# FoX attention over the paged past: K tiles read by indirect transfers on GpSimd, in one order with V

## The reference

```python
past = (_gather_pages(cache_fox_k[i], page_table),
        _gather_pages(cache_fox_v[i], page_table),
        _gather_pages(cache_fox_logf[i], page_table))
...
k_all = jnp.concatenate([pk.astype(k.dtype), k], axis=1)
v_all = jnp.concatenate([pv.astype(v.dtype), v], axis=1)
...
s = jnp.einsum('bqhd,bkhd->bhqk', q_i, k).astype(f32) * ATTN_SCALE
s = s + jnp.transpose(cq_i, (0, 2, 1))[..., None] - cum_k_t[:, :, None, :]
s = jnp.where(k_idx[None, None, None, :] <= pos_i[None, None, :, None], s, -jnp.inf)
pr = jax.nn.softmax(s, axis=-1)
return jnp.einsum('bhqk,bkhd->bqhd', pr.astype(v.dtype), v)
```

## Time and profile before

| | us |
|---|---|
| median of 3 runs | 2632.93 |
| lowest, highest | 2631.06, 2641.93 |
| the profiled execution | 2635.9 |
| its span | 2634.1 |
| mean granted clock of TensorE in it | 0.915 |

### The profile page before, as it was taken

The page is one execution under the profiler, slowest core; times in us unless marked ns, Lnnn a source line. Parts: engine busy times, 40 slices in busy tenths (PEclk is TensorE's granted clock), DMA queues, the critical chain, the costliest instruction groups (busy, mean ns, idle before and its releaser), DMA issues. The chain is left out here.

```text
span 2634.1 us, 63573 instructions
## 1 busy us (share of the span) xinstructions
PE 2263.2 (86%) x26373; PEld 1761.8 (67%) x26373; DVE 1437.3 (55%) x2317; ACT 868.8 (33%) x1577; POOL 380.8 (14%) x512
## 2 busy tenths in 40 slices
PE   6798888887977997889999979998777776999998
PEld 3565777776746873667777757655766655777776
DVE  2436777775565546565422264557666657453333
ACT  2335444442241222333322231156433323333222
POOL 2003233331000000111100000024222310111000
PEclk8899899998977977899999989999888888999999
DMA  7423899996350015123323324452999931332331
GB/s 245 113 77 126 301 358 361 357 352 237 89 193 18 4 43 186 49 73 88 91 78 97 89 71 137 137 160 68 283 286 287 285 92 34 94 88 80 89 89 60
DMA packets 309226, 392.64 MB, mean 149 GB/s; under 512 B 26240, under 2 KB 227274, under 8 KB 308964
## 3 DMA queue, kind: packets, MB, share of 16 engines
q1 hardware_dynamic: 277892, 282.16, 34.9%
q0 software_dynamic: 31072, 106.72, 12.3%
HBM read 378.11 MB, written 10.70 MB: 148 GB/s over the span
## 5 line engine op out<-in xcount | busy, mean ns | idle before, releaser
L837 PE MATMUL bank<-yT,WH 128*128 128x288 f16 x3200 | 532.3, 290 | 45.8 <-DVE yT L691 34.6
L837 PEld LDWEIGHTS bank<-yT,WH 128*128 128x128 f16 x3200 | 314.2, 99 | 144.6 <-issue 48.7
L901 DVE SCALAR_TENSOR_TENSOR WL<-wring,WH 128x1024 f16<-128x1024 f32 x194 | 255.5, 1321 | 257.8 <-ACT WH L881 257.6
L1384 DVE TENSOR_TENSOR KL<-bank,KH 128x512 f16<-128x512 f32 x416 | 278.0, 687 | 179.4 <-ACT KH L1364 153.1
L1364 ACT CAST KH<-bank 128x512 f16<-128x512 f32 x416 | 238.5, 585 | 364.4 <-PE bank L1282 349.8
L837 PE MATMUL bank<-uT,WH 128*128 128x288 f16 x2048 | 337.9, 288 | 10.6 <-DVE WL L901 10.6
L837 PE MATMUL bank<-yT,WL 128*128 128x288 f16 x1600 | 331.5, 289 | 0.0
L881 ACT ACTIVATE WH<-wring 128x1024 f16<-128x1024 f32 x194 | 203.5, 1054 | 267.1 <-PE bank L837 221.1
L837 PEld LDWEIGHTS bank<-uT,WH 128*128 128x128 f16 x2048 | 201.6, 99 | 63.3 <-DVE WL L901 11.2
L837 PE MATMUL bank<-uT,WL 128*128 128x288 f16 x1024 | 210.8, 288 | 0.0
L837 PE MATMUL bank<-hT,WH 128*128 128x288 f16 x960 | 163.3, 294 | 29.1 <-DVE hT L728 18.7
(11 more groups left out here) (457 smaller groups left out, 4010.5 us busy)
## 6 DMA issues: line engine op xcount, KB each, us to landing
wring<-in_ada_w SPq DMA_DIRECT2D x96, 512.0 KB, 4.9
vTd<-in_state_dil_k SPq DMA_DIRECT2D x160, 256.0 KB, 9.3
vslot<-in_state_dil_v POOLq DMA_DIRECT2D x156, 256.0 KB, 9.0
yT<-in_cache_fox_k SPq DMA_DIRECT2D x128, 256.0 KB
krows<-in_cache_fox_k SPq DMA_DIRECT2D x128, 256.0 KB
wring<-in_mlp_up SPq DMA_DIRECT2D x64, 512.0 KB, 4.0
wring<-in_mlp_down SPq DMA_DIRECT2D x64, 512.0 KB, 3.9
wring<-in_ev_w_in SPq DMA_DIRECT2D x26, 512.0 KB, 3.9
```

The source lines that it names most:

```text
L837: last = nc.tensor.matmul(bank[b + h][:, 0:HALF], w[s % 2][:, c, :], x[:, s % parts * KC + c, h * HALF:(h + 1) * HALF], start=(s % parts = ...
L901: nc.vector.scalar_tensor_tensor(WL[s % 2][:, :, :], w[:, :, :], WSCALE, WH[s % 2][:, :, :], ALU.mult, ALU.subtract).then_inc(w_free, 1)
L1384: nc.vector.tensor_tensor(KL[i][:, :], turned[n % NT][:, :], KH[i][:, :], ALU.subtract).then_inc(lo_out, 1)
```

## The change

K tiles are read like V tiles: by one indirect DMA on GpSimd with the row numbers of `vrow_of` (`load_pair` in place of `load_page` and the two loaders of V). Each such DMA raises its semaphore by 16, so `LANDED` is 16 again.

`attend_past` gets `one_queue`. With it SyncE issues nothing in the stage, and GpSimd runs through `keys_and_values`: K tiles in order from 4 on, after the first three K tiles two V tiles each until V2 to V7 are issued, later V tile t - 15 behind K tile t, the partition maximum of sequence s ahead of K tile 16s + 21, and at the end the last V tiles, four of them between others into the K buffers. `late` is empty then. `take_k` and `reduce_max` are the former lines as functions; without `one_queue` (the second layer) nothing is different.

In `attend_prompt` GpSimd reads K0, K1, V0 and V1 in step U = 2, and after its last step `pool_last` waits for the stores and reads K2 and K3. SyncE does nothing there.

```diff
--- before.py
+++ after.py
@@ -1029,7 +1029,7 @@
         store(sp, prompt_out.rearrange("(t p) n -> p t n", p=P), rows[:, 0:NTILE, :])
         store(sp, sample_out, rows[0:NDEC, NTILE, :])
 
-    def attend_prompt(npairs, qT, kT, vrows, chunk0, bias_of, scope, S, PT, late_mask=None, out_room=None, on_sp=None, on_pool=None):
+    def attend_prompt(npairs, qT, kT, vrows, chunk0, bias_of, scope, S, PT, late_mask=None, out_room=None, on_sp=None, on_pool=None, pool_last=None):
         NU = 4 * npairs
         SR = len(S)
         nmx = sb(scope, "nmx", [P, SR, 2])
@@ -1177,9 +1177,11 @@
                         pool.wait_ge(sum_ok, pr)
                     for h in range(2):
                         nc.gpsimd.tensor_scalar(DG[h][:, qt, :], ident, rinv[:, U % SR, h:h + 1], None, ALU.mult).then_inc(dg_ok, 1)
-
-
-    def attend_past(nt, E, TU, KR, VR, LEAD, chunk0, Q, KNEW, VNEW, load_k, load_v, bias_of, new_bias_of, K_home, k_in, V_home=(), v_first=(), LANDED=16, V_LANDED=16):
+                if pool_last:
+                    pool_last(pool)
+
+
+    def attend_past(nt, E, TU, KR, VR, LEAD, chunk0, Q, KNEW, VNEW, load_k, load_v, bias_of, new_bias_of, K_home, k_in, V_home=(), v_first=(), LANDED=16, V_LANDED=16, one_queue=False):
         QB, QH, QL = Q
         SG = 4
         nu = nt * TU
@@ -1223,7 +1225,7 @@
             def used_up_to(t):
                 return ((t + 1) * TU + SG - 1) // SG
 
-            late = {x: sem(f"v_late{x}") for x in range(VR + KR, nt) if x % 2 == 1}
+            late = {x: sem(f"v_late{x}") for x in range(VR + KR, nt) if x % 2 == 1 and not one_queue}
 
             def v_home(t):
 
@@ -1249,23 +1251,55 @@
                 dst, landed, _ = v_home(t)
                 load_v(eng, t, dst, landed)
 
+            def take_k(eng, t):
+                eng.wait_ge(kt_ok, (t - KR + 1) * TU)
+                load_k(eng, t, K[t % KR], k_in[t % KR])
+
+            def reduce_max(pool, s):
+                pool.wait_ge(cmx_ok, 2 * s + 2)
+                nc.gpsimd.partition_all_reduce(amx[:, s % 2, :], cmx[:, s % 2, :], P, RMAX).then_inc(amx_ok, 1)
+
+            def keys_and_values(pool):
+
+
+                behind = VR + (VLAG - 2 * VR - 6) // 2 + 1
+                spread = len(V_home)
+                for t in range(KR, NT_ + nt):
+                    s, x = divmod(t - nt - KR - 1, nt)
+                    if x == 0 and s >= 0:
+                        reduce_max(pool, s)
+                    if t < NT_:
+                        take_k(pool, t)
+                    while spread < min(VR, len(V_home) + 2 * (t - KR + 1)):
+                        take_v(pool, spread)
+                        spread += 1
+                    v = t - behind
+                    if VR <= v < LAST + VR:
+                        take_v(pool, v)
+                    if 0 <= t - NT_ < KR:
+                        take_v(pool, LAST + VR + t - NT_)
+                for x in range(VR + KR, nt):
+                    take_v(pool, LAST + x)
+
             with nc.Block() as block:
                 @block.sync
                 def _(sp):
+                    if one_queue:
+                        return
                     for t in range(KR, NT_):
-                        sp.wait_ge(kt_ok, (t - KR + 1) * TU)
-                        load_k(sp, t, K[t % KR], k_in[t % KR])
+                        take_k(sp, t)
                     for x in range(VR, nt):
                         if x < VR + KR or x in late:
                             take_v(sp, LAST + x)
 
                 @block.gpsimd
                 def _(pool):
+                    if one_queue:
+                        keys_and_values(pool)
+                        return
                     for t in range(NT_):
                         if t % nt == VR - 1:
-                            s = t // nt
-                            pool.wait_ge(cmx_ok, 2 * s + 2)
-                            nc.gpsimd.partition_all_reduce(amx[:, s % 2, :], cmx[:, s % 2, :], P, RMAX).then_inc(amx_ok, 1)
+                            reduce_max(pool, t // nt)
                         x = t - LAST
                         if t >= len(V_home) and (x < VR or (x >= VR + KR and x not in late)):
                             take_v(pool, t)
@@ -1507,35 +1541,26 @@
             k_in = [sem(f"k_in{i}") for i in range(4)]
             v_first = [sem(f"v_in{i}") for i in range(2)]
 
-            def load_page(cache):
-                src = I[cache][0].rearrange("n p h d -> n p (h d)")
-
-                def load(eng, n, dst, done):
-                    for a in range(2):
-                        page = eng.value_load(pt_sb[0:1, 2 * n + a:2 * n + a + 1], min_val=0, max_val=319)
-                        eng.dma_start(dst[a:P:2, :], src[ds(page, 1), :, :].rearrange("a (p e) n -> (a p) (e n)", e=2)).then_inc(done, 16)
+            def load_pair(cache):
+
+                rows = I[cache][0].rearrange("n (p e) h d -> (n p) (e h d)", e=2)
+
+                def load(pool, n, dst, done):
+                    nc.gpsimd.indirect_dma_start(dst[:, :], None, rows, bass.IndirectOffsetOnAxis(ap=vrow_of[:, n:n + 1], axis=0),
+                                                 bounds_check=320 * PAGE // 2 - 1, oob_is_err=False).then_inc(done, 16)
                 return load
-            load_k, load_v_pages = load_page("cache_fox_k"), load_page("cache_fox_v")
-            v_rows = I["cache_fox_v"][0].rearrange("n (p e) h d -> (n p) (e h d)", e=2)
-
-            def load_v(eng, n, dst, done):
-
-                if eng is nc.sync:
-                    load_v_pages(eng, n, dst, done)
-                else:
-                    nc.gpsimd.indirect_dma_start(dst[:, :], None, v_rows, bass.IndirectOffsetOnAxis(ap=vrow_of[:, n:n + 1], axis=0),
-                                                 bounds_check=320 * PAGE // 2 - 1, oob_is_err=False).then_inc(done, 16)
-
-            def first_reads(sp):
+            load_k, load_v = load_pair("cache_fox_k"), load_pair("cache_fox_v")
+
+            def first_reads(pool):
                 for t in range(2):
-                    load_k(sp, t, K_home[t], k_in[t])
-                all_stored(sp)
-                for t in range(2, 4):
-                    load_k(sp, t, K_home[t], k_in[t])
-
-            def first_values(pool):
+                    load_k(pool, t, K_home[t], k_in[t])
                 for t in range(2):
                     load_v(pool, t, V_home[t], v_first[t])
+
+            def last_reads(pool):
+                all_stored(pool)
+                for t in range(2, 4):
+                    load_k(pool, t, K_home[t], k_in[t])
             with ExitStack() as sc:
                 qkT = sb(sc, "qkT", [P, 8, TOK])
                 vrows = sb(sc, "vrows", [P, 5, 512])
@@ -1653,13 +1678,13 @@
                 turn_rows([(vT, 0, 4, lambda t: vrows[:, t, :]), (qkT, 4, 4, lambda t: krows[:, t, :])], {"pe": pe_extra, "dve": dve_extra, "act": act_extra, "sp": stores})
                 attend_prompt(4, qkT[:, 0:4, :], qkT[:, 4:8, :], vrows, 4, lambda h, n: NB[:, h, 0:n], sc,
                               [sb(sc, f"S{i}", [P, 2, NPR]) for i in range(3)], [sb(sc, f"PT{i}", [P, 2, 13, P]) for i in range(2)], C["causal"],
-                              on_sp=first_reads, on_pool=first_values)
+                              on_sp=lambda sp: None, on_pool=first_reads, pool_last=last_reads)
 
             def bias_of(vs, t0, n):
                 v = decay[:, vs, :, t0:t0 + n].rearrange("p h t -> p t h")
                 return v.unsqueeze(3).to_broadcast([P, n, 8, 8])
             attend_past(PAGES // 2, 1, 2, 4, 8, 2, 4, (QB, QH, QL), KNEW, VNEW, load_k, load_v, bias_of,
-                        lambda s: nbias[:, s, :, :], K_home, k_in, V_home, v_first, LANDED=32)
+                        lambda s: nbias[:, s, :, :], K_home, k_in, V_home, v_first, one_queue=True)
 
 
     def rwkv():
```

## The result

The changed kernel took 2731.98 us (median of four executions, 2729.81 to 2734.8) where the kernel before took 2637.43 on that chip (four, 2631.06 to 2646.32): ratio 1.0357, 95% interval 1.032 to 1.0393. The forecast was 2629 and the range ended at 2653. The same program, run again later on another chip, took 2625.74 us (ten executions, 2617.95 to 2635.45) beside 2623.35 for the kernel before: ratio 1.0018, interval 0.9994 to 1.0043. The program's executions fall into two conditions, and in one of them TensorE is held up: it pauses, inside its steps too, for no reason that the code gives. The first result fell into it. I call it the holding condition, the other the free one.

What follows compares the result with a forecast made beforehand. SyncE's K issue was taken to pace the early stretch, and K's arrival the 400 GB/s stretches, softmax work the slow ones. From 2635.9 us, -4 - 4 + 1 + 0 = -7 gave 2629 us, range 2608 to 2653.

Steps and rivals of the forecast that it cites:

- Can one queue carry it all?: Stage's DMA: one queue moves 380 to 401 GB/s, 5.2 to 5.5 us per pair of tiles, under today's 5.85.
- the added part: Stage: 124 more indirect DMAs on GpSimd at 1.31 us make its load 5.39 us per pair against 5.85, 92% busy.
- Rival (E): Stage: VectorE stretches GpSimd's descriptor writing, a pair costs 6.67 us, total 2673 us; chance 0.05.
- Load of GpSimd and one queue: Stage: GpSimd needs 5.39 us a pair, 1.31 us back to back; one queue gives 380 to 401 GB/s.
- (B): Stage: nearly all waiting for K goes, -21 us, 2615 us, K issues every 5.4 us per pair; chance 0.28.
- First reads: Prompt attention's end: K0 to K3 reads on GpSimd hide in TensorE's work and GpSimd's 6.06 us wait; zero.
- The partition maximum: GpSimd, once per sequence: K and V issues ahead of it may delay VectorE; +1 us over eight sequences, bounds 0 and +27.
- Early and steady stretch: Early: K tiles every 2.1 us instead of 2.53, -4 us; steady: shorter waits for K, -4 us, bounds -17 and +2.
- The tail: Stage's end, last V tiles: GpSimd ends the last at 626.5 us, as SyncE did; zero, bounds -1 and +2.

Runs made afterwards that it cites:

- half_k_indirect: The changed kernel with only even K tiles by indirect DMA on GpSimd, odd ones by page transfers on SyncE; 2658.3 us.
- v_on_sync: The changed kernel with V tiles moved to page transfers on SyncE, K still indirect on GpSimd; 2624.6 us.
- v_on_sync_first_k_too: v_on_sync with K tiles 0 to 3 read by SyncE, as in the kernel before; 2628.6 us, ratio 1.0016.
- early_maximum_again: The changed kernel with one more partition maximum, of a constant, on GpSimd ahead of the first reads of K2 and K3; 2626.7 us.
- after_third: The changed kernel itself, unaltered, run a third time on one more chip; 2735.0 us.
- small_indirect: k_on_sync with 124 indirect reads of 32 bytes a partition added on GpSimd, one at each place of a K transfer; 2789.8 us.
- k_on_sync: The changed kernel with K tiles read again by SyncE's page transfers, V indirect on GpSimd in the new order; 2625.6 us, later timed at 2629.8, ratio 0.9965.
- gpsimd_compute: k_on_sync with a 128 x 224 elementwise multiply added on GpSimd at each place of a K transfer; 2678.1 us.

## Why the prediction was wrong

The step that failed stands in "Can one queue carry it all?" and in the added part: 124 indirect DMAs were charged to GpSimd (1.31 us each) and to the DMA engines, and nothing to TensorE. In the holding condition they cost TensorE 398.0 - 297.4 = 101 us in slots 44 to 255, 0.8 us each on average. It isn't a price of each: for half of them it was 35 us (half_k_indirect), and in v_on_sync, which has K's transfers but not V's on GpSimd, nothing (293.2 us). No row of the trace of before could have given that price, but a sign was there: 17.1 us of "issue" waits on TensorE's own lines, in a stage whose other waits I had listed.

```profile
PE bank L1293 <- issue: 8.4, 15, 1.3
PE bank L1282 <- issue: 5.6, 9, 1.1
PE bank L1295 <- issue: 1.6, 4, 0.5
PE bank L1294 <- issue: 1.5, 3, 0.5
```

I took them for noise. Most of it (14.0 us) stands at L1293 and L1282, whose first matmul has a wait in the code in front of it; only the 3.1 us at L1294 and L1295 are plainly inside a step.

That the free condition gave 2625.7 us, near the forecast of 2629, is luck and no hit: the forecast was 7 us less than the kernel before, and beside the kernel before there it was 2.4 us more (interval -1.6 to +11).

**Rival (E)** had the right operation and the wrong victim. GpSimd's transfers weren't stretched: the fastest and the median V transfer are where they were in the earlier trace rows.

```profile
L1549 POOL DMA_INDIRECT vslot<-in_cache_fox_v,vrow_of x62: 986/990/1573, 262.2 to 620.0; - x62
```

So the trap of the Trainium skill (SBUF — State Buffer, "SBUF: two separate sides"), by which VectorE can lock GpSimd out of writing descriptors, is not what happened; VectorE's instructions beside it kept their length too (KL at 688 ns on average in both conditions).

**Load of GpSimd and one queue: right, seen in the free condition.** Back to back it stayed at 1.29 us. GpSimd ran 196 indirect transfers and 6 maxima in 270 us, which fills some 260 of them, near the 5.39 us a pair that was worked out as its load. The queue gave 383 GB/s against an estimate of 380 to 401. The pace was 5.56 us a pair (293.1 us for 211 slots, four to a pair), between the 5.7 to 5.8 of the forecast and the 5.4 of (B). TensorE waited 18.9 us for K from 330 to 600 us, where less than 17 had been named as the sign (14.5 before in that stretch), and GpSimd, in chains of up to 32, waited little for TensorE: it set the pace more than the forecast had it. The Trainium skill's sentence that all issuers share the same 16 engines (DMA: Bandwidth & Descriptors, "Issuing engines are not separate DMA queues") agrees with that row: 383 GB/s by one issuer, where two had 375 in the same condition (v_on_sync_first_k_too) and 358 in the earlier trace rows.

**First reads: wrong, +2 us.** K2 and K3 were put into GpSimd's wait for the end of the block. But the block's end waits for GpSimd. TensorE began the stage at 245.72 before and at 248.94 now, 4.9 us after GpSimd's last issue:

```profile
243.02 1.00 POOL L1549 DMA_INDIRECT krows<-in_cache_fox_k,vrow_of  x1 [0.30 <-issue]
248.94 2.79 PE L1316 MATMUL bank<-cst,yT 128*128 128x128 f32 x12 [4.07 <-PEq L1045]
```

In early_maximum_again GpSimd ended at 249.18 and TensorE began at 253.98, again 4.8 us later; over the eight traces in which GpSimd reads K2 and K3 there by indirect transfers it is 4.2 to 5.1 us. Not all of the 3.2 us between the two starts comes from this. From TensorE's last matmul of the block before to its first of the stage it is 2.0 us in the kernel before and in all others that read K2 and K3 on SyncE, and 3.4 to 4.2 us in the seven that read them on GpSimd and have no early maximum: 1.4 to 2.2 us. The rest lies in the spread of the work ahead. I had taken the 6.06 us of the earlier trace rows for idle time that could be filled.

**The partition maximum: +1 was too little.** The first one costs GpSimd 6.89 us in which nothing is seen, before it can run:

```profile
293.79 1.00 POOL L1549 DMA_INDIRECT yT<-in_cache_fox_k,vrow_of  x1 [1.24 <-PE bank L1316]
301.68 0.54 POOL L1260 PARTITION_ALL_REDUCE amx<-cmx  x1 [6.89 <-issue]
```

VectorE waited 4.6 us for it, and the stretch from 294 to 306 us moved 109 GB/s. In the kernel before GpSimd had waited 38.56 us ahead of its first maximum and started it 0.14 us after VectorE's `cmx`, against 4.66 us here: a preparation of that length had room inside the wait and cost nothing. Moving the K issues over took the cover away. The Trainium skill has it (GPSIMD Engine Reference, "2.1 Instruction dispatch": the first call to a freshly loaded kernel pays a load of about 6 us, with no visible instruction); the trace agrees at 6.89 and, in the free condition, 6.74 us. In early_maximum_again the gap was gone and slots 0 to 44 took 56.3 instead of 62.1 us, but the load now stood in front of K2 and K3 and the stage began 7 us later: the ratio was 1.0028 against 1.0018.

**Early and steady stretch.** With the load of the first maximum out of the way (early_maximum_again) slots 0 to 44 took 56.3 us against 57.6 before: 1 us gained, where 4 had been forecast. From slot 44 to 255 the free trace is 14 us shorter than the one of before, but that one is of the holding condition, and there is no trace of the kernel before in the free one. Worked out from the whole: +2.4 us, less some 2 for the first reads and 6 for the first maximum, leaves about -6 for the two stretches, against -8 forecast. That is an argument from two medians whose interval is 6 us wide either way, so it isn't shown. **The tail**, from slot 255 to the end of the last values step, took 21.0 us before, 22.7 now and 20.6 in the free condition: no loss there, as forecast.

**What stays open** is what the holding condition is. In it and out of it the program is the same, and so are the fetches of instructions by their length (16 KB each, 29 and 39 from 330 to 600 us, 1.0 us each); 96 holds don't fit 29 fetches. The DMA packets are not quite the same. One of 4 KB takes 159 ns at the median in both, but 192 against 169 ns on average, and the slowest tenth 211 ns and more against 166 (after_third: 197 and 240), although fewer bytes move. In small_indirect it is 198 ns on average, in k_on_sync 170. So packets are slow where TensorE is held; which of the two comes first, or whether a third thing does both, no run shows. Nor is it clear why half_k_indirect, with as many second places in a chain (42) as the kernel before (40), lost 25 us in the slots beside it: its "issue" waits are hardly longer (19.5 against 17.1 us), but the gaps within values steps added up to 67 us against 46, most of them too short to count as waits.

## What to carry to other kernels

A loss that falls inside an engine's steps, under "issue" and without a wait in the code, is not explained by the schedule; run the unchanged kernel again beside the next experiment before believing a cure, best on another chip. Before filling GpSimd's idle time, see what it covers: here its wait for the end of a block was not free, since the block's end waited for it, and the wait ahead of the first partition maximum covered a preparation of 6 to 7 us. And where two issuers share the load at no cost, as SyncE and GpSimd did here, one issuer for both wins little (in the free condition nothing) and can lose 3.6% (in the holding one).

## What the runs showed of the hardware

- Two conditions, seen on different chips and on one chip at different times: in one, TensorE's instructions pause for 0.15 to 1.2 us at a time beside dense indirect transfers on GpSimd (96 pauses in 270 us; 106 at the values step alone in small_indirect), in the other hardly ever (1 in 270 us), beside chains of 32. Time 2732 against 2626 us for one program.
- In the changed kernel under the holding condition the waits grow with the place in a chain of back-to-back indirect transfers: 0.04 us for each first one, 0.19 for each second and third, 0.91 for each fourth.
- The pause doesn't depend on the bytes (32 a partition or 4 KB), nor on the partitions (16 or 128). With plain transfers or arithmetic on GpSimd in their place there were 2.2 and 4.5 us of "issue" waits.
- DMA packets of 4 KB took 192 and 197 ns on average in the two traces of the changed kernel with pauses and 169 ns in the one without, 159 ns at the median in all.
- Ahead of a partition maximum that follows another kind of arithmetic on GpSimd it stood idle for 7.5 us on average (five in gpsimd_compute); after indirect transfers only the first one had such a gap.
- The next block's first matmul came 4.2 to 5.1 us after GpSimd's last indirect transfer of the block before, where that read K2 and K3 (eight traces).
